# Gate and up columns of a float32 FFN: one 512-column matmul for two of 256, the two halves added on VectorE

## What is computed

```python
def swiglu(x, w_gate, w_up, w_down):
    return (jax.nn.silu(x @ w_gate) * (x @ w_up)) @ w_down
```

## Time and profile before

| | us |
|---|---|
| median of 3 runs | 2382.7 (2377.88, 2382.7, 2382.9) |
| the profiled execution's own time | 2381.7 |
| its span | 2380.0 |
| TensorE (PE) busy | 2183.3 (92%) |
| PE weight load (PEld) busy | 1520.7 (64%) |
| VectorE (DVE) busy | 914.5 (38%) |
| ScalarE (ACT) busy | 728.4 (31%) |
| GpSimd (POOL) busy | 76.4 (3%) |
| the three FFN gate/up lines L2115 to L2117, PE busy | 1196.1, 4224 matmuls |

### The profile page before, as it was taken

The page is one execution under the profiler, slowest core; times in us unless marked ns, Lnnn a source line. Parts: engine busy times, 40 slices in busy tenths (PEclk is TensorE's granted clock), DMA queues, the critical chain, the costliest instruction groups (busy, mean ns, idle before and its releaser), DMA issues.

```text
span 2380.0 us, 29460 instructions
## 1 busy us (share of the span) xinstructions
PE 2183.3 (92%) x12373; PEld 1520.7 (64%) x12373; DVE 914.5 (38%) x1211; ACT 728.4 (31%) x952; POOL 76.4 (3%) x102
## 2 busy tenths in 40 slices
PE   8869999998775999999869998999999999998999
PEld 6454343333364433433329997878998998787998
DVE  4750000000466100000035546745455455764554
ACT  4621000000253100000024334744334334464332
POOL 2000000000000000000010002000000000200000
PEclk9979999999897999999989999999999999999999
DMA  7189999999817999999986554316554554414551
GB/s 262 45 349 381 421 421 421 421 421 421 328 63 297 389 421 421 421 421 421 421 325 198 179 185 148 105 58 193 186 185 159 187 185 149 148 54 148 188 182 65
DMA packets 194811, 618.34 MB, mean 260 GB/s; under 512 B 10568, under 2 KB 119248, under 8 KB 145552
## 3 DMA queue, kind: packets, MB, share of 16 engines
q1 hardware_dynamic: 192432, 612.01, 67.6%
q0 software_dynamic: 2272, 4.81, 0.8%
HBM read 615.73 MB, written 1.05 MB: 259 GB/s over the span
## 4 chain that ended last, share of the span: by engine, by line
PE 72%; DMA 14%; DVE 8%; ACT 3%; DVEq 2%; issue 1%; ACTq 0%; SPq 0%
PE W L1953 18%; PE W L2115 7%; PE W L2117 7%; PE W L2116 7%; DMA moe_own<-in_moe_w 6%; DMA moe_split<-in_moe_w 5%; PE acc L1838 4%; PE acc L1839 4%; PE acc L1842 4%; PE W L1800 3%; PE W L1801 3%; PE W L1802 3%; DMA raw<-in_moe_w 2%; PE W L1937 2%; PE acc L1946 2%; DVE w_lo L1106 1%
## 5 line engine op out<-in xcount | busy, mean ns | idle before, releaser
L1106 DVE TENSOR_TENSOR w_lo<-raw,w_hi 128x2048 fp32r<-128x2048 f32 (+2 forms) x216 | 457.3, 2121 | 448.9 <-ACT w_hi L686 447.7
L686 ACT ACTIVATE w_hi<-raw 128x2048 fp32r<-128x2048 f32 (+2 forms) x216 | 382.7, 1773 | 534.7 <-PE W L2117 303.8
L2115 PE MATMUL W<-xT_hi,w_hi 128*128 128x256 f32 x1408 | 399.3, 284 | 1.1 <-DVE xT_lo L1138 1.1
L2117 PE MATMUL W<-xT_hi,w_lo 128*128 128x256 f32 x1408 | 398.4, 283 | 0.0
L2116 PE MATMUL W<-xT_lo,w_hi 128*128 128x256 f32 x1408 | 398.4, 283 | 0.0
L1372 DVE TENSOR_TENSOR hid<-W,hid 128x512 f32<-128x512 f32 x32 | 22.1, 692 | 741.3 <-PE W L1953 741.3
L2115 PEld LDWEIGHTS W<-xT_hi,w_hi 128*128 128x128 f32 x1408 | 270.0, 192 | 3.2 <-issue 1.6
L2116 PEld LDWEIGHTS W<-xT_lo,w_hi 128*128 128x128 f32 x1408 | 270.1, 192 | 1.4
L2117 PEld LDWEIGHTS W<-xT_hi,w_lo 128*128 128x128 f32 x1408 | 270.1, 192 | 0.0
L1800 PE MATMUL W<-w_hi,xT_hi 128*128 128x474 f32 (+1 forms) x400 | 157.0, 393 | 16.1 <-DVE w_lo L1106 14.3
L1953 PE MATMUL W<-moe_split,xe 128*64 128x512 f32 x672 | 153.1, 597 | 10.5 <-DMA moe_split<-in_moe_w 9.1
(11 more groups left out here) (360 smaller groups left out, 2660.5 us busy)
## 6 DMA issues: line engine op xcount, KB each, us to landing
moe_own<-in_moe_w SPq DMA_DIRECT2D x120, 1024.0 KB, 26.4
moe_split<-in_moe_w SPq DMA_DIRECT2D x120, 1024.0 KB, 26.6
raw<-in_moe_w SPq DMA_DIRECT2D x108, 1024.0 KB, 26.4
raw<-in_ffn_w_gate SPq DMA_DIRECT2D x44, 1024.0 KB, 5.3
raw<-in_ffn_w_up SPq DMA_DIRECT2D x44, 1024.0 KB, 5.3
raw<-in_ffn_w_down SPq DMA_DIRECT2D x44, 1024.0 KB, 4.9
moe_xt<-in_moe_w SPq DMA_DIRECT2D x36, 1024.0 KB, 26.4
raw<-in_w_in SPq DMA_DIRECT2D x32, 948.0 KB, 4.9
```

The lines of the kernel that those rows point to most:

```text
L686: s.activation(w_hi[split_slot(c)][:, 0:cols], raw[slot_of(c)][:, 0:cols], ACT.Copy).then_inc(hi_ready, 1)
L1106: v.tensor_tensor(w_lo[split_slot(c)][:, 0:cols], raw[slot_of(c)][:, 0:cols], w_hi[split_slot(c)][:, 0:cols].bitcast(F32), ALU.subtract).t ...
L2115: t.matmul(out, hi, xT_hi[:, kc, :], start=(kc == 0), stop=False)
L2117: return t.matmul(out, lo, xT_hi[:, kc, :], start=False, stop=(kc == KC - 1))
```

## The change

The lower half of x is laid right behind the upper one, and one matmul of 512 columns multiplies the upper weights by both halves at once (L2133 of the new kernel); its result is two runs of 256 sums in one whole bank. The lower weights by the upper half (L2134) are still a matmul of 256 columns, into the first run. Since one `f` half of one chunk now fills a bank, gate and up of both halves take all four banks of `W`. The order within a group becomes gate `f`=0, up `f`=0, gate `f`=1, up `f`=1. VectorE adds the two runs of each bank with a `tensor_reduce` over an axis of length two (the halves lie 256 elements apart) into SBUF, `silu` reads that sum, and all of `silu` and `hidden` works on 128x256 pieces, twice per group. `used` of both chunks is now signalled in the second half of the group.

```diff
-        xT_hi = at("xT_hi", [P, KC, SEQ], F32R)
-        xT_lo = at("xT_lo", [P, KC, SEQ], F32R)
+        xT_both = at("xT_both", [P, 2, KC, SEQ], F32R)
+        xT_hi, xT_lo = xT_both[:, 0], xT_both[:, 1]
...
-        sg = at("sg", [P, 2, 512])
-        hb = at("hb", [P, 512])
+        gate_sum = at("gate_sum", [P, 2, SEQ])
+        up_sum = at("up_sum", [P, 2, SEQ])
+        sg = at("sg", [P, 2, SEQ])
+        hb = at("hb", [P, 2, SEQ])
...
 ScalarE
-            def ffn(c0, last):
-                def silu(parity, consumed):
-                    act.wait_ge(used, consumed.v)
-                    s.activation(sg[:, parity, :], W[:, 2 * parity, :], ACT.Silu).then_inc(ff["sg"], 1)
+            def ffn(c0, g0, last):
+                def silu(n):
+                    for f in range(2):
+                        act.wait_ge(ff["gate"], (n + (f + 1)).v)
+                        s.activation(sg[:, f, :], gate_sum[:, f, :], ACT.Silu).then_inc(ff["sg"], 1)
+
+                silu(g0)
                 split(c0 + 3)
-                silu(0, c0 + 1)
                 split(c0 + 4)
                 with act.Fori(0, (FF_GROUPS - 3) // 2) as i:
                     for t in range(2):
                         c = (c0 + (2 + 3 * t)).plus(i, 6)
+                        silu((g0 + 2 * (t + 1)).plus(i, 4))
                         split(c + 3)
-                        silu(1 - t, c + 1)
                         split(c + 4)
                         split(c + 5)
...
 VectorE
+                def sums(f, ready_gate, ready_up):
+                    dve.wait_ge(*ready_gate)
+                    v.tensor_reduce(gate_sum[:, f, :], W[:, 2 * f, :].rearrange("p (h t) -> p t h", h=2), AX, ALU.add).then_inc(ff["gate"], 1)
+                    dve.wait_ge(*ready_up)
+                    v.tensor_reduce(up_sum[:, f, :], W[:, 2 * f + 1, :].rearrange("p (h t) -> p t h", h=2), AX, ALU.add)
                     v.drain().then_inc(ff["h"], 1)
+
+                def hidden(parity, f, n):
+                    dve.wait_ge(ff["sg"], (n + (f + 1)).v)
+                    v.tensor_tensor(hb[:, f, :], up_sum[:, f, :], sg[:, f, :], ALU.mult)
                     v.drain()
+                    hi, lo = hT_hi[:, parity, f, :], hT_lo[:, parity, f, :]
+                    v.tensor_copy(hi, hb[:, f, :])
+                    v.drain()
+                    v.tensor_tensor(lo, hb[:, f, :], hi.bitcast(F32), ALU.subtract)
                     v.drain().then_inc(ff["hT"], 1)
 
+                def first_columns(parity, n):
+                    sums(0, (ff["first"], (n + 1).v), (ff["first"], (n + 2).v))
+                    hidden(parity, 0, n)
+
+                def second_columns(parity, n, c):
+                    sums(1, (used, (c + 1).v), (used, (c + 2).v))
+                    hidden(parity, 1, n)
+
+                first_columns(0, g0)
+                second_columns(0, g0, c0)
                 rest(c0 + 3)
                 rest(c0 + 4)
-                hidden(0, c0 + 2, sg0 + 1)
                 with dve.Fori(0, (FF_GROUPS - 3) // 2) as i:
                     for t in range(2):
                         c = (c0 + (2 + 3 * t)).plus(i, 6)
+                        n = (g0 + 2 * (t + 1)).plus(i, 4)
+                        first_columns(1 - t, n)
+                        second_columns(1 - t, n, c)
                         rest(c + 3)
                         rest(c + 4)
-                        hidden(1 - t, c + 2, (sg0 + (t + 2)).plus(i, 2))
                         rest(c + 5)
...
 TensorE
-                def up(c, bank, first=False):
-                    pe.wait_ge(lo_ready, (c + 1).v)
+                def columns(c, f, bank, first=False):
                     hi, lo = w_hi[split_slot(c)], w_lo[split_slot(c)]
+                    for kc in range(KC):
+                        if first:
+                            wait_block(call, 0, kc)
+                        cols = slice(kc * FF_COLS + f * P, kc * FF_COLS + (f + 1) * P)
+                        wide, narrow = W[:, bank, :].rearrange("p (h t) -> p h t", h=2), W[:, bank, 0:SEQ]
+                        if kc < KC - 1:
+                            t.matmul(wide, hi[:, cols], xT_both[:, :, kc, :], start=(kc == 0), stop=False)
+                            t.matmul(narrow, lo[:, cols], xT_hi[:, kc, :], start=False, stop=False)
+                        else:
+                            t.matmul(narrow, lo[:, cols], xT_hi[:, kc, :], start=False, stop=False)
+                            last = t.matmul(wide, hi[:, cols], xT_both[:, :, kc, :], start=False, stop=True)
+                    return last
+
+                def up(c, n, first=False):
                     for f in range(2):
-                        for kc in range(KC):
-                            if first and f == 0:
-                                wait_block(call, 0, kc)
-                            cols = slice(kc * FF_COLS + f * P, kc * FF_COLS + (f + 1) * P)
-                            last = exact_w(W[:, bank, f * SEQ:(f + 1) * SEQ], hi[:, cols], lo[:, cols], kc)
-                    last.then_inc(used, 1)
+                        if not first:
+                            pe.wait_ge(ff["h"], (n + (f + 1 - 2)).v)
+                        for i in range(2):
+                            if f == 0:
+                                pe.wait_ge(lo_ready, (c + (i + 1)).v)
+                            columns(c + i, f, 2 * f + i, first and f == 0 and i == 0).then_inc(used if f else ff["first"], 1)
...
                 def group(c, j_par, n, first):
-                    pe.wait_ge(ff["h"], n.v)
-                    up(c, 2 * (1 - j_par))
-                    up(c + 1, 2 * (1 - j_par) + 1)
+                    up(c, n)
                     down(c + 2, j_par, n, first, False)
```

More of the change, by code:

```diff
@@ L343, in build_program @@
         od = {n: sem("od_" + n) for n in ("pad", "tp", "tr", "xc", "hi", "lo", "gates", "ri", "nla", "exp", "m2", "sqrt", "h", "out_hi", "done", "sp", "sp2")}
-        rt = {n: sem("rt_" + n) for n in ("logitsT", "logits_sb", "logits", "max", "exp", "chosen", "ranks", "counts", "ready")}
+        rt = {n: sem("rt_" + n) for n in ("logitsT", "logits_sb", "logits", "max", "exp", "chosen", "ranks", "ready")}
         me = {n: sem("me_" + n) for n in ("pick", "ga", "xe", "pt", "pte", "sg", "h", "tr", "hT", "y", "sc")}
@@ L348, in build_program @@
         rm = {n: sem("rm_" + n) for n in ("ssd", "std", "rs", "xa", "xd", "acc0", "x0", "x1a")}
-        ff = {n: sem("ff_" + n) for n in ("sg", "h", "hT")}
-        mx = {n: sem("mx_" + n) for n in ("in", "sq", "ss", "std", "ng", "copied", "blank", "qkp", "qkd", "dup", "qkt", "qkta", "is", "relu",
-                                          "bias", "wide", "decay", "decay_sb", "z", "e", "ln", "nlf", "s", "sb", "p", "t", "te", "o", "at", "x", "cg", "ib")}
+        ff = {n: sem("ff_" + n) for n in ("first", "gate", "sg", "h", "hT")}
+        mx = {n: sem("mx_" + n) for n in ("in", "sq", "ss", "std", "copied", "blank", "qkp", "qkd", "dup", "qkt", "qkta", "is", "relu",
+                                          "bias", "wide", "decay", "decay_sb", "z", "ln", "s", "sb", "p", "t", "te", "o", "at", "cg", "ib")}
         ov = [{n: sem(f"ov{i}_" + n) for n in ("landed", "free", "tensor", "scalar", "vector")} for i in range(DEPTH)]
@@ L963, in ffn @@
                         i = 2 + 3 * (FF_GROUPS - 3 + t) + k
+                        if k == 0:
+                            silu(g0 + 2 * (FF_GROUPS - 2 + t))
                         if i + AHEAD < FF_CHUNKS or not last:
                             split(c0 + (i + AHEAD))
-                        if k == 0:
-                            silu(1 - t, c0 + (i + 1))
             def mixer(l, c0):
@@ L1081, in _ @@
                 split(c0 + (AHEAD - 1))
-                ffn(c0 + C_FFN1, False)
+                ffn(c0 + C_FFN1, N(0, (l, 4 * FF_GROUPS)), False)
                 for b in range(TB):
@@ L1198, in _ @@
             v.memset(bxT[:, :, 0:CONV_B - 1], 0.0)
-            v.drain().then_inc(ff["h"], 1)
-            dve.sem_inc(ev["pad"], 1)
+            v.drain().then_inc(ev["pad"], 1)
             dve.wait_ge(x_in, 16)
@@ L1537, in ffn @@
                         c = (c0 + (2 + 3 * t)).plus(i, 6)
+                        n = (g0 + 2 * (t + 1)).plus(i, 4)
+                        first_columns(1 - t, n)
+                        second_columns(1 - t, n, c)
                         rest(c + 3)
                         rest(c + 4)
-                        hidden(1 - t, c + 2, (sg0 + (t + 2)).plus(i, 2))
                         rest(c + 5)
                 for t in range(2):
+                    i = 2 + 3 * (FF_GROUPS - 3 + t)
+                    n = g0 + 2 * (FF_GROUPS - 2 + t)
+                    first_columns(1 - t, n)
+                    second_columns(1 - t, n, c0 + i)
                     for k in range(3):
-                        i = 2 + 3 * (FF_GROUPS - 3 + t) + k
-                        if i + AHEAD < FF_CHUNKS or not last:
-                            rest(c0 + (i + AHEAD))
```

(10 more changed lines are left out.)

31 lines of the change are left out of this document (11 added, 20 removed).

## The result

| | us |
|---|---|
| before, median of 8 runs | 2380.51 (2377.1 to 2384.33) |
| changed, median of 8 runs | 2386.43 (2385.16 to 2388.11) |
| ratio | 1.0024, interval 1.0014 to 1.0035 |
| the profiled execution's own time, and its span | 2386.19, 2384.3 |

The change makes the kernel 5.9 us slower. That is 0.24%, just above what can be told from no change. The forecast was 2379.5, 3.2 us faster than before, and "within 0.2%".

What follows compares the result with a forecast made beforehand. TensorE's stream of matmuls was taken to bound the FFNs. From 2381.7, minus 16.8 for merging plus 13.6 for stalls gave 2378.5, or 2379.5 us against the median 2382.7; range 2371 to 2391.

Steps and rivals of the forecast that it cites:

- What the change gives on TensorE: FFN matmuls: merging saves 0.0119 us at each of 1408 upper weight block uses, 16.8 us in all.
- the favourable rival: FFN matmuls: alternating wide and narrow shrinks the fixed part, gain 27 us, 2369 us; chance 0.12.
- The stalls: Start of each FFN: TensorE waits 1.4 us, then 2.0 us for lower weights; 13.6 us over four FFNs.
- The clock: Behind the new FFN-start stalls: the granted clock may fall, 1.7 us lost each; the forecast counted none.
- its rival: FFN starts: clock falls at the new stalls, four give 2386.3, all eight 2393.1; decides from the fifth; chance 0.06.
- VectorE's sums: Steady FFN groups: four reduces of 0.69 us each stay hidden behind `down`, with 0.7 us to spare.
- the rival of the slow reduce: VectorE's PSUM sums: up to 1.56 us each instead of 0.69, giving 2389.1; decides at about 1.4 us; chance 0.10.
- `silu` and `split` in time: ScalarE in FFN groups: `silu`, 0.50 us at most, and `split` finish without delaying TensorE.
- the wait for `hT` worth nothing: End of a layer's first FFN: `down`'s 0.9 us wait, twice in all, goes but gains 0.
- Saves nothing: FFN merged matmul: two runs cost a start each, 0.2398 us, leaving only stalls, 2396.3 us; chance 0.10.
- Smaller fixed part where they take turns: FFN matmuls: narrow weights load behind 512 columns, so the gain is 27 us, 2369 us; chance 0.12.

Runs made afterwards that it cites:

- in blocks: Changed kernel with all eight merged matmuls of a half chunk first, then all eight narrow ones; 2380.97 us, ratio 1.0004 to the kernel before.
- gate first: Changed kernel with both gate halves before both up halves, and `rest` between gate and up sums; 2372.2 us, again 2369.22; ratios 0.9956, 0.9953 to the kernel before.

## Why the prediction was right or wrong

**The verdict.** The time, 2386.43, lies in the range, but the forecast of "within 0.2%" was wrong: the chance given to slower was 0.26. The shape of the account held (a gain in the steady groups, eaten by the starts), and two terms of the sum were off, both in the same direction: -3.2 us were forecast, and 5.4 for the price of the merged matmuls, 0.6 for the restarts and 3.0 for the falls of the clock bring it to +5.8, where +5.9 was measured. That it meets so closely is in part luck, since unchanged code alone moves the time by more than that.

- *The term that failed: "What the change gives on TensorE", -16.8.* It came to -11.4. The prices of the two kinds were right by themselves: in blocks a pair costs 0.348, and the period is 16.61 against 16.60. The step that failed took each from a stream of its own kind and added them for a stream where they take turns. There the pair costs 0.3525, not 0.3478, and the saving per place is 0.0072 us, not 0.0119; `down`, 0.03 us shorter per group (5.44 for 5.47), gives a part of it back. The text saw that wide and narrow take turns, and drew only the favourable rival from it. Worth 5.4 us, this is the larger miss.
- *The stalls: right.* 1.4 and 2.0 us were forecast, 1.39 and 1.95 measured, in all four FFNs. Missing was the restart, 0.10 us a stall: 14.2 instead of 13.6. That the second comes from the place of `rest` in VectorE's list is shown by the `rest` moved ahead of the last sum, which removed it alone. The first comes from TensorE's new order, which wants the up chunk after half of the gate chunk: with the old order in gate first it is gone too.
- *The clock: right as a mechanism, wrong in the sum.* The forecast took no fall, its rival counted from the fifth on. In the profiles one or two of the four long stalls are followed by one (eight of 16 in the four profiles with stalls of 1.8 us), 1.5 us each where 1.7 was forecast; the shorter stalls by none. The sum needed the expected number, about +3 us, not the likeliest case of none, even though each fall alone was no case of its own. With it and the turns, the forecast would have read -11.4 + 14.2 + 3.0 = +5.8, and 2388.5 against the median that was shown (five more runs put the median of before at 2380.51, 2.2 lower).
- *VectorE's sums: hidden, as said.* The reduce takes 692 ns where 690 was taken, so the rival of the slow reduce falls. The spare is 0.60 us where 0.7 was forecast. One number of that rival was off as well: by its own terms it decides at about 1.5 us, not 1.4 (0.83 us over 0.69 cost 3.3 at the starts and 4.7 in the groups, which with the -3.2 make 4.8).
- *`silu` and `split` in time, and the wait for `hT` worth nothing: right.* `silu` takes 418 ns, under the bound of 0.50.
- *"Saves nothing": wrong as a mechanism.* Reading x in one run of 512 changed nothing (period 16.72), so two runs cost no start. But part of its effect was there, because the two kinds take turns.
- *"Smaller fixed part where they take turns": the opposite holds.*

The Trainium skill ("PSUM — Partial Sum Buffer", section "Specifications (TRN2)") warns of non-contiguous patterns in matmuls; for VectorE's reads of pairs 256 elements apart the rows here show no cost at all, 692 against 690 ns.

## What to carry to other kernels

A change that makes the steady loop faster by a fraction of a microsecond can lose it all at the loop's start, so read the first two rounds of the new order by themselves: which buffer is wanted earlier than before, and what stands ahead of its producer on the producer's own engine. Moving that producer into an idle time of its engine removed the second stall; with TensorE's old order as well, which removes the first, gate first turned a loss of 6 us into a gain of 11. Price a mix of instructions from a row of the same mix where there is one, and otherwise bound the mix from both sides; count a stall of TensorE in a dense stream with its restart and its share of falls of the clock; and where the rest of the kernel scatters by more than the change is worth, compare the changed stretch alone, profile by profile.

## What was not expected of the hardware

- Matmuls of 512 and of 256 columns, each with its own weights, cost 0.3525 us a pair when they take turns and 0.348 in blocks of eight; by the group it is 16.72 against 16.61 us. The moving operand in two runs or one makes no difference.
- The first matmul behind a stall of TensorE costs 0.10 us more (0.33 to 0.34 to the next start, for 0.24 by turns), and this is also how a wait shows that has no idle time in the profile.
- The granted clock fell to 0.50 behind a stall of 1.80 us within a stream that was dense on both sides in 8 of 16 cases, in the profile shown once immediately and once some 1.5 us later, and cost 1.5 us; behind 1.24 us in none of 28, behind 2.55 in two of 4 and behind 3.32 in four of 4.
